# Two SwiGLU layers: one 512-column product for both parts of x, and a new order of the small work beside it

## The reference, cut to what matters

```python
FFN_HIDDEN = 2816
def swiglu(h, w_gate, w_up, w_down):
    return (jax.nn.silu(h @ w_gate) * (h @ w_up)) @ w_down
```

## Time and profile before

| | before |
|---|---|
| median of 3 runs | 1988.35 us |
| the profiled execution's own time | 1988.46 us |
| its span | 1986.7 us |
| granted clock of TensorE, mean | 0.989 |
| TensorE busy | 1897.9 us, 96% |
| VectorE busy | 1384.1 us, 70% |
| ScalarE busy | 990.0 us, 50% |
| GpSimd busy | 257.1 us, 13% |

### The profile page before, as it was taken

One profiled execution on the slowest core, in us unless ns is written; L12 is line 12 of the kernel. 1 busy time (PEld: TensorE's weight loads), 2 busy tenths in 40 slices (PEclk: granted clock), 3 DMA queues, 4 the chain that ended last, 5 costly groups with the idle time before them and its releaser, 6 DMA issues.

```text
span 1986.7 us, 33458 instructions
## 1 busy us (share of the span) xinstructions
PE 1897.9 (96%) x13306; PEld 1751.9 (88%) x13306; DVE 1384.1 (70%) x2518; ACT 990.0 (50%) x1442; POOL 257.1 (13%) x118
## 2 busy tenths in 40 slices
PE   6989899999988999999999899999999999999998
PEld 6887799999968799999898799999988888999997
DVE  5897775558957773347666559988878887666665
ACT  5645544455435554455555445566653334444444
POOL 0001044440001034430000065000000000000000
PEclk8999999999999999999999999999999999999999
DMA  8754467765564255545434354577766866465452
GB/s 319 245 189 142 150 237 258 258 225 199 183 229 154 97 194 181 188 170 201 166 129 168 111 175 161 184 219 215 219 206 255 301 240 231 179 231 193 174 208 107
DMA packets 94553, 391.96 MB, mean 197 GB/s; under 512 B 7680, under 2 KB 41776, under 8 KB 56000
## 3 DMA queue, kind: packets, MB, share of 16 engines
q1 hardware_dynamic: 94112, 389.58, 56.4%
q10 hardware_dynamic: 288, 0.26, 0.1%
HBM read 371.72 MB, written 15.73 MB: 195 GB/s over the span
## 4 chain that ended last, share of the span: by engine, by line
PE 77%; DVE 11%; ACT 3%; issue 2%; DMA 1%; POOL 0%; ACTq 0%; DVEq 0%; SPq 0%
PE ps L569 10%; PE ps L571 10%; PE ps L570 10%; PE acc L565 9%; PE acc L566 9%; PE acc L567 9%; PE acc L569 3%; PE acc L570 3%; PE acc L571 3%; DVE wlo L1345 2%; PE ps L1300 1%; PE acc L1300 1%; DVE arena L1374 1%; PE ps L1043 1%; PE ps L714 1%
## 5 line engine op out<-in xcount | busy, mean ns | idle before, releaser
L2400 ACT ACTIVATE whi<-raw 128x1024 fp32r<-128x1024 f32 x557 | 588.7, 1060 | 484.7 <-PE acc L567 273.1
L1345 DVE TENSOR_TENSOR wlo<-raw,whi 128x1024 fp32r<-128x1024 f32 x461 | 569.2, 1242 | 292.6 <-ACT whi L2400 289.5
L569 PE MATMUL ps<-hhi,whi 128*128 128x256 f32 x1848 | 527.3, 285 | 7.0 <-DVE wlo L1345 3.1
L571 PE MATMUL ps<-hhi,wlo 128*128 128x256 f32 x1848 | 522.8, 283 | 0.0
L570 PE MATMUL ps<-hlo,whi 128*128 128x256 f32 x1848 | 522.7, 283 | 0.0
L569 PEld LDWEIGHTS ps<-hhi,whi 128*128 128x128 f32 x1848 | 354.1, 192 | 12.9 <-issue 4.1
L570 PEld LDWEIGHTS ps<-hlo,whi 128*128 128x128 f32 x1848 | 354.3, 192 | 2.8
L571 PEld LDWEIGHTS ps<-hhi,wlo 128*128 128x128 f32 x1848 | 354.1, 192 | 0.0
L1345 POOL TENSOR_TENSOR wlo<-raw,whi 128x1024 fp32r<-128x1024 f32 x96 | 239.8, 2501 | 616.6 <-ACT whi L2400 616.4
L565 PE MATMUL acc<-whi,chi 128*128 128x512 f32 x752 | 296.0, 394 | 3.5 <-DVE wlo L1345 1.9
L566 PE MATMUL acc<-whi,clo 128*128 128x512 f32 x752 | 294.5, 392 | 0.0
(11 more groups left out here) (452 smaller groups left out, 2399.7 us busy)
## 6 DMA issues: line engine op xcount, KB each, us to landing
raw<-in_peer_down SPq DMA_DIRECT2D x64, 1024.0 KB, 5.0
raw<-in_peer_up SPq DMA_DIRECT2D x64, 1024.0 KB, 5.0
arena<-in_ada SPq DMA_DIRECT2D x80, 512.0 KB, 5.1
raw<-in_w_gate SPq DMA_DIRECT2D x22, 1024.0 KB, 4.8
raw<-in_w_up SPq DMA_DIRECT2D x22, 1024.0 KB, 4.8
raw<-in_w_down SPq DMA_DIRECT2D x22, 1024.0 KB, 4.8
arena<-spill SPq DMA_DIRECT2D x14, 1024.0 KB, 7.0
spill<-hT_t SPq DMA_DIRECT2D x22, 448.0 KB, 5.9
```

The source lines that it names most:

```text
L569: e.matmul(out, hi, xh, start=start, stop=False, skip_group_check=True)
L571: i = e.matmul(out, lo, xh, start=False, stop=stop, skip_group_check=True)
L1345: e.tensor_tensor(out=lo, in0=w, in1=hi.bitcast(F32), op=ALU.subtract).then_inc(*X(("lo", j)))
L2400: e.activation(hi, w, ACT.Copy, scale=1.0).then_inc(*self.A(("hi", j)))
```

## The change

Three things. First, `hhi` and `hlo` become one tensor `hpair`, viewed as `hP`, in which the high and the low part of a tile of x are 2048 columns apart, and in gate and up the two products of the high weights become one product of 512 columns, which writes 256 sums for each part of x; the product of the low weights stays, with 256 columns, onto the first half. A gate or up step then needs two banks of its four instead of one, and VectorE must add the two halves of each bank. Second, these sums: `ve_halves`, four a step, each a `tensor_reduce` over pairs, from PSUM to SBUF; gate's two stand right behind VectorE's low parts up to U0 or U1, ahead of the low part of D0 or D1, and silu and the product by up then work from SBUF. Third, the high and low parts of the next step's first block stand ahead of the activation's product and copy.

```diff
@@ Memory
-        hhi, hlo = sb("hhi", [128, 2048], F32R), sb("hlo", [128, 2048], F32R)
+        hpair = sb("hpair", [128, 4096], F32R)
+        self.hP = hpair[:, :].rearrange("p (s a t) -> p a s t", s=2, a=8)
+        self.hH, self.hL, ... = self.hP[:, :, 0, :], self.hP[:, :, 1, :], ...
-        self.act = alloc(1024, 4, T)
+        self.act, self.up = alloc(1024, 4, T), alloc(512, 2, T)
@@ TensorE
+    def pe_mm2(self, e, ps, tile, k, *keys):
+        hi, lo, end = tile
+        e.matmul(ps.rearrange("p (s t) -> p s t", s=2), hi, self.m.hP[:, k], start=k == 0, stop=False, ...)
+        i = e.matmul(ps[:, 0:T], lo, self.m.hH[:, k, :], start=False, stop=k == 7, ...)
+    def pe_linear_halves(self, e, name, i, split=None):
+        self.pe_ada(e)
+        if split:
+            for j in range(2):
+                self.banks.take(e, name, i, j)
+        for n in range(16):
+            j, k = (n % 2, n // 2) if split else (n // 8, n % 8)
+            if split and j == 0:
+                self.pe_split(e, split, k)
+            if not split and k == 0:
+                self.banks.take(e, name, i, j)
+            self.pe_mm2(e, ..., k, *([("full", name, i, j)] if k == 7 else []))
@@ VectorE
+    def ve_halves(self, e, dst, *key):
+        src = self.banks.tile(*key)[:, :].rearrange("p (s t) -> p t s", s=2)
+        e.wait_ge(*self.at("full", *key))
+        e.tensor_reduce(out=dst, in_=src, axis=AX, op=ALU.add, negate=False).then_inc(...)
             self.ve_linear(e, f"w_gate{layer}", i, 8, 2)
+            for j in range(2):
+                self.ve_halves(e, m.act[:, s.start + j, :], f"w_gate{layer}", i, j)
             self.ve_linear(e, f"w_up{layer}", i, 8, 2)
-            e.wait_ge(*self.at("out", f"w_gate{layer}", i))
-            e.wait_ge(*self.at("full", f"w_up{layer}", i))
-            e.tensor_tensor(out=m.act[:, s, :], in0=m.act[:, s, :], in1=pu, op=ALU.mult)...
+            for j in range(2):
+                self.ve_halves(e, m.up[:, j, :], f"w_up{layer}", i, j)
+            e.wait_ge(*V.last)
+            self.cut_lo(e, V, self.W.last(f"w_up{layer}", 16 * i + 15) + 3)
+            e.wait_ge(*self.at("silu", layer, i))
+            e.tensor_tensor(out=m.act[:, s, :], in0=m.act[:, s, :], in1=m.up, op=ALU.mult)...
@@ ScalarE
             self.se_linear(e, f"w_gate{layer}", i, 8, 2)
-            self.se_linear(e, f"w_up{layer}", i, 8, 2)
-            ... silu of gate's bank ...
+            self.cut_hi(e, self.W.last(f"w_up{layer}", 16 * i + 15) + 1)
+            e.wait_ge(*self.at("out", f"w_gate{layer}", i, 1))
+            e.activation(m.act[:, s, :], m.act[:, s, :], ACT.Silu, scale=1.0).then_inc(*A(("silu", layer, i)))
+            self.cut_hi(e, self.W.last(f"w_up{layer}", 16 * i + 15) + 3)
+            e.wait_ge(*self.at("act", layer, i))
```

More of the change, by code:

```diff
@@ L300, in tiles8 @@
             return ap[:, :].rearrange("p (a t) -> p a t", a=8)
-        self.hH, self.hL, self.cH, self.cL = tiles8(hhi), tiles8(hlo), tiles8(chi), tiles8(clo)
+        self.hP = hpair[:, :].rearrange("p (s a t) -> p a s t", s=2, a=8)
+        self.hH, self.hL, self.cH, self.cL = self.hP[:, :, 0, :], self.hP[:, :, 1, :], tiles8(chi), tiles8(clo)
         self.hT = tiles8(self.hT_t)
@@ L573, in pe_mm3 @@
             i.then_inc(*self.P(*keys))
+    def pe_mm2(self, e, ps, tile, k, *keys):
+        hi, lo, end = tile
+        if end is not None:
+            keys = (*keys, ("used", end))
+        e.matmul(ps.rearrange("p (s t) -> p s t", s=2), hi, self.m.hP[:, k], start=k == 0, stop=False, skip_group_check=True)
+        i = e.matmul(ps[:, 0:T], lo, self.m.hH[:, k, :], start=False, stop=k == 7, skip_group_check=True)
+        if keys:
+            i.then_inc(*self.P(*keys))
     def pe_split(self, e, split, k):
@@ L594, in pe_linear @@
                         xl[:, k, :], n == 0 if split else k == 0, k == kt - 1, *keys)
+    def pe_linear_halves(self, e, name, i, split=None):
[9 more added lines that the diff above has]
+                self.banks.take(e, name, i, j)
+            self.pe_mm2(e, self.banks.tile(name, i, j), self.W.tile(e, name, (2 * i + j) * 8 + k), k,
+                        *([("full", name, i, j)] if k == 7 else []))
     def pe_linear_tok(self, e, name, i, kt, xh, xl, split=None, ada=True):
@@ L927, in pe_ffn @@
         for i in range(11):
-            self.pe_linear(e, f"w_gate{layer}", i, 8, 2, m.hH, m.hL, None if i else f"ffn{layer}")
-            self.pe_linear(e, f"w_up{layer}", i, 8, 2, m.hH, m.hL)
+            self.pe_linear_halves(e, f"w_gate{layer}", i, None if i else f"ffn{layer}")
+            self.pe_linear_halves(e, f"w_up{layer}", i)
             if i:
@@ L1375, in ve_ada @@
                                            op1=ALU.add).then_inc(*V(*([("ada", s)] if k else [])))
+    def ve_halves(self, e, dst, *key):
+        src = self.banks.tile(*key)[:, :].rearrange("p (s t) -> p t s", s=2)
+        e.wait_ge(*self.at("full", *key))
+        e.tensor_reduce(out=dst, in_=src, axis=AX, op=ALU.add, negate=False).then_inc(*self.V(("out", *key)))
     def ve_pieces(self, e, n):
@@ L1804, in ve_ffn @@
             self.ve_linear(e, f"w_gate{layer}", i, 8, 2)
+            for j in range(2):
+                self.ve_halves(e, m.act[:, s.start + j, :], f"w_gate{layer}", i, j)
             self.ve_linear(e, f"w_up{layer}", i, 8, 2)
-            e.wait_ge(*self.at("out", f"w_gate{layer}", i))
-            e.wait_ge(*self.at("full", f"w_up{layer}", i))
-            pu = self.banks.tile(f"w_up{layer}", i)[:, 0:512].rearrange("p (a t) -> p a t", a=2)
-            e.tensor_tensor(out=m.act[:, s, :], in0=m.act[:, s, :], in1=pu, op=ALU.mult).then_inc(
-                *V(("out", f"w_up{layer}", i)))
+            for j in range(2):
[3 more added lines that the diff above has]
+            e.wait_ge(*self.at("silu", layer, i))
+            e.tensor_tensor(out=m.act[:, s, :], in0=m.act[:, s, :], in1=m.up, op=ALU.mult).then_inc(*V(("act", layer, i)))
             e.wait_ge(*self.at("hi", f"act{layer}", i))
```

## The result

The changed kernel takes 1990.62 us (median of 22 runs, 1987.43 to 1995.21), the kernel before 1987.36 in the same comparison (22 runs). The ratio is 1.0021, 95% interval 1.0014 to 1.0028: slower by 4.2 us (2.8 to 5.6; the two medians are 3.3 apart), at the edge of the 0.2% that the prediction called measurable, where 1981 had been forecast. The profiled execution took 1990.89 us.

A forecast was written before the change was run, and what follows sets the result against it. TensorE's rate was taken to bound the FFNs. From 1988.46 us, -10.9 + 2.2 + 1.7 + 0.2 + 0.4 - 0.9 = -7.3 gave 1981.2, by the median 1981.0; range 1975 to 1991.

The forecast's parts named there:

- products, 704 tiles: Gate and up of both FFNs: a tile falls from 0.360 to 0.3445 us, saving 10.9 us, between 8.4 and 13.4.
- lock behind steps 2 and 4: First FFN, U0': if GpSimd gets the shared lock first, TensorE stalls 2.2 us; 2.2 in all, bounds 0 and 4.5.
- step 1: First FFN: VectorE's backlog makes D0 1.4 us late and G1' of step 2 another 0.3; together 1.7 us.
- gate 7, with the clock: First FFN, small products ahead of gate 7: no wait and no slow clock were forecast, 0 us.
- behind gate 0: Second FFN: TensorE already waits for the modulation behind gate 0, so gate 0's 0.2 us of gain are lost.
- first tail, second tail: Ends of the FFNs: first loses 0.4 us at down 10's late low part; second wins 0.9 us at `gate_g`.
- rival (b): First FFN: VectorE becomes the bound if a sum costs 1.4 us; 15 us more, 1996 in all; chance 12%.
- the one on the extra pieces: First FFN: steps 2 and 4 have an uncovered extra modulation piece; at 6 and 8 products L714 give 0.9 us more.
- my walk: Working that times each VectorE and GpSimd operation of a first-FFN step from t = 0, VectorE seeing up's last product.
- the two-piece operand: Gate and up: taken as free; rival (a), 16%, had each piece cost, losing 8.4 us of gain, about 1989.5.
- The even odds: U0' behind steps 2 and 4: GpSimd or VectorE gets the lock, margin 0.1 to 0.2 us, even odds for each.
- the sums at 0.69 us: VectorE's 88 sums of halves in both FFNs: taken at 0.69 us each, bounds 0.54 and 1.4.

The follow-up runs named there:

- e3_pieces: Changed kernel with the modulation's extra pieces at steps 2, 4, 5, 8 instead of 2, 4, 6, 8; ratio 1.0011 to the kernel before.
- e5_order: Kernel before with only the new order in both FFNs, next gate block's parts ahead of the activation's work, old products and silu; ratio 1.0037 to before.
- e4_contig: Changed kernel with the high and low part of a tile of x side by side in `hpair`, one piece of 512 columns; ratio 1.0022 to before.
- e13_grouped: Changed kernel with the old order in the first FFN and products of two tiles grouped 512, 512, 256, 256 in both; ratio 1.0028 to before.
- e16_second_grouped: Kernel before with the change in the second FFN alone, products of two tiles grouped 512, 512, 256, 256; 1982.16 us, ratio 0.9965 to before.
- e2_small_sums: Changed kernel with VectorE's sums over 8 columns instead of 256 from step 2 on; ratio 1.0017 to the kernel before.
- e14_no_extra: Changed kernel without the modulation's four extra pieces at steps 2, 4, 6 and 8, left to the first FFN's end; 1992.68 us, ratio 1.0025 to before.
- e15_before_no_extra: Kernel before without the modulation's four extra pieces at steps 2, 4, 6 and 8; 1998.24 us, ratio 1.0052 to before.
- e10_late0: Changed kernel with the old order in the first FFN alone, new products and sums in both; ratio 1.0053 to the kernel before.
- e8_parity: Changed kernel with VectorE and GpSimd exchanged for the low parts in the first FFN; ratio 1.0015 to the kernel before.
- e9_parity_pieces: Changed kernel with VectorE and GpSimd exchanged in the first FFN and extra pieces at steps 2, 4, 5, 8; ratio 0.9999 to before.
- e12_late_both: Changed kernel with the old order in both FFNs, new products and sums kept; ratio 1.0082 to the kernel before.

## Why the prediction was wrong

| term | forecast | measured |
|---|---|---|
| products, 704 tiles | -10.9 | -5.7 |
| lock behind steps 2 and 4 | +2.2 | +3.8 |
| step 1 | +1.7 | +1.5 |
| gate 7, with the clock | 0 | +4.6 |
| behind gate 0 | +0.2 | +0.2 |
| first tail, second tail | +0.4, -0.9 | +0.6, -0.5 |
| sum | -7.3 | +4.5 |

The products' -5.7 is what is left of the two stretches once their waits are taken out: 194.05 - 187.45 - 9.9 = -3.3 and 182.62 - 185.35 - 0.2 + 0.5 = -2.4. The pair without extra pieces gives 185.03 - 186.51 - 1.7 = -3.2 for the first. It is a remainder, so it also takes up what a wait really costs above or below its recorded length, and down's 0.03 us a step. The sum stands beside a measured difference of 2.8 to 5.6. Slower had a chance of 0.12, all of it for rival (b), whose cause didn't come about.

**The step that failed in its mechanism** is the one on the extra pieces: "They have an extra piece with nothing on TensorE beside it (at 6 and 8 the products L714 give 0.9 us more)." I counted L714 as cover. They are also a customer: they stand ahead of gate 7 and need the very piece that GpSimd's earlier low part stretches from 1.54 to 3.51 us. In my walk that piece ended at t + 7.95, and TensorE comes to gate 7 at t - 0.27 + 5.47 = t + 5.2. Both numbers stood in the working and their difference is 2.75, near the 3.07 measured; but I asked of each block only whether its low part was ready, not whether the small products ahead of it had their input. e3_pieces shows the cause directly: with the piece a step earlier the wait is gone. e5_order shows what moved the piece into GpSimd's low part: the new order alone gives 3.03 us there, without the sums. The slow clock behind the stall, which the prediction has no term for, is 1.5 of the 4.6 us; e5_order's stall of 3.03 did without it.

**The term that was mis-sized** is the products. 0.3445 us a tile came from places in the earlier trace rows where 256 columns follow 512 once, between down and gate; in a steady alternation a tile takes 0.353, above the 0.348 of my range, and down loses 0.03 a step. e4_contig rules out the two-piece operand, e13_grouped and e16_second_grouped show that the order of sizes alone gives back 0.15 of 11.29 us. What in TensorE makes the difference, and why some blocks of the changed kernel keep 0.346, stays open. The shortfall is 5.2 us, as large as that of gate 7.

**The even odds** at U0' both fell to GpSimd. In each of the five meetings read (296.22, 354.59, 330.39, 261.21 and, within a piece, 363.88) its request came 0.3 to 0.6 us before VectorE's running operation ended, and it went next each time. In all sixteen profiles no low part of GpSimd takes over 3.35 us, against 2.38 alone, and no operation of VectorE with both inputs in SBUF began and ended while one was under way: GpSimd never stood back for a second operation. That is all that these runs show of who wins. On that, my walk's 9.35 against 9.53 should have been read as lost.

**Right:** the sums at 0.69 us (rival (b) falls; e2_small_sums shows their length doesn't matter from step 2 on), and their staying out of the lock (all 88 take 0.67 to 0.69 us, also beside a running low part of GpSimd) while the activation's product joins it (2.42 us instead of 0.69 at 730.69, where GpSimd began at 730.17); the wait in step 1 near D0 with 1.27 and 0.21 for 1.7, the loss behind gate 0, and the first tail, 0.6 us for 0.4. `gate_g`'s wait fell from 1.18 to 0.65, not under 0.4.

## What to carry to other kernels

When work moves on an engine with a shared lock, list for each operation behind it everyone who waits: small products in the middle of a block as well as the next block's weights; cover and customer can be the same instruction. On the lock that VectorE and GpSimd share, GpSimd, asking while an operation of VectorE ran, went next in every case here, so a low part right behind a chain of short operations is the one that loses. A change that is good in itself can lose by the slack that other work was hidden in: test it without that work, as e14_no_extra and e15_before_no_extra do, and put it where there is none. And before a difference of a few us is read from one profile, count where its granted clock fell: the same stall can bring a fall in one execution and none in the next.

## What the runs showed of the hardware that I had not expected

- Whether the granted clock falls behind a short stall of TensorE doesn't go by the stall's length: it fell behind 2.16 us in e5_order and 2.42 in e2_small_sums, and stayed at 1.00 behind 2.43 in the changed kernel, 2.88 in e10_late0 and 3.03 in e5_order. A stall of 2.67 us brought a fall in e8_parity and none in e9_parity_pieces, and of the three alike stalls in the first FFN one brought a fall in e10_late0 and all three in e12_late_both. A fall costs some 1.5 us, so that a stall can cost half as much again as its length.
- Alternating products of 512 and 256 columns take 0.353 us a tile, grouped by size 0.348, though columns and weight loads are the same, and the same alternation runs at 0.346 in some blocks.
